# One stage for both Hyena convolutions and the neighbourhood attention, in 64 steps

## The chip, the cores and the metric

The kernel runs on one core of a Trainium2 chip. The metric is the time of the device for one execution, in microseconds. TensorE multiplies matrices, VectorE (DVE), ScalarE (ACT) and GpSimd (POOL) work on elements, SyncE (SP) and POOL issue DMA transfers. The engines meet through semaphores only; each runs its own program in order.

## The reference, cut to what matters

The reference is a chain of two transformer blocks; the change touches the last layer's two mixers. Everything is fp32.

```python
def two_sided_fftconv(u, h_f, h_b):
    kern = jnp.concatenate([h_f, jnp.zeros_like(h_f[:1]), h_b[1:][::-1]], axis=0)
    uf = jnp.fft.rfft(u, n=2 * l, axis=1)
    kf = jnp.fft.rfft(kern, axis=0)
    return jnp.fft.irfft(uf * kf[None], n=2 * l, axis=1)[:, :l]
...
        z = v
        for o, g in enumerate((x1, x2)):
            z = g * (two_sided_fftconv(z, filt[:, o, 0], filt[:, o, 1]) + z * hy_bias[o])
```

There are 1024 positions and 512 channels. The second convolution (order 1) takes the result of the first (order 0).

```python
def neighbourhood_attention(q, k, v, k_ctx, v_ctx, rpb):
    s_rows = jnp.einsum('bhrqd,bhrwkd->bhrwqk', qg, k_rows)
    s_win = (s_win + bias[None])...
    s_ctx = jnp.einsum('bhrqd,bhcd->bhrqc', qg, k_ctx)
    p = jax.nn.softmax(jnp.concatenate([s_win, s_ctx], axis=-1).astype(F32), axis=-1)
    out = jnp.einsum('bhrwqk,bhrwkd->bhrqd', p_rows, v_rows) + jnp.einsum('bhrqc,bhcd->bhrqd', p_ctx, v_ctx)
```

The 1024 latent tokens form a grid of 16 rows and 64 columns, in 8 heads of 64. A query sees a window of 8 rows (512 keys, masked to 16 columns by the bias) and 256 context keys. The two mixers do not depend on each other: both read what the stage before (the projection "g_odd") wrote, and the last projection ("proj3") reads both.

## The kernel before

`program` (L3853) runs a list of stages. Each has its own tiles, semaphores and engine programs (`stage`, L34), and ends with a barrier of all engines once its stores have landed. The three stages concerned come one after another, between `odd_stage` and the last `project_stage` (L3913 to L3917).

`conv_stage` (L3443), run twice. The transform is a product with cosine and sine tables. The input z is held as even and odd positions (r = 0, 1), four tiles of 128 each, 512 channels wide. Forward (L3507 to L3517): for each of four blocks f of 128 frequencies, for cosine and sine (n) and both r, four fp32 matmuls of 128x128 by 128x512 accumulate over t; 16 matmuls per f. ScalarE copies the odd sums out of PSUM (L3540); VectorE makes sum and difference (L3548, L3549), multiplies by the filter's spectrum KS (L3559) and combines (L3562, L3563); POOL mixes the results into Y (L3494, L3495). Inverse (L3519 to L3530): for each of four t and both r, eight fp32 matmuls over f and n; TensorE waits for `mixed` before the first. VectorE adds the bias term (L3572, L3576) and multiplies by the gate (L3578); POOL stores (L3500). The result goes to HBM as Z1, and the second convolution loads it from there. SP loads one table of 1 MB per f or t, in two buffers.

`na_stage` (L3596). Keys and queries of all heads are loaded and transposed first (L3689, L3736, L3738). Then 64 steps: one step u is one grid row of one pair of heads. The queries of both heads stand block-diagonally in a 128x128 tile `qbd` (L3762), so that one matmul of 512 window keys and one of 256 context keys give the scores of both heads (L3703, L3704). VectorE adds the bias (L3787), copies the context scores (L3788) and takes the negated maximum (L3791). ScalarE takes the exponential and its sum (L3751). TensorE transposes the probabilities in six pieces (L3710), ScalarE copies them to SBUF (L3748), TensorE weighs the values in six matmuls of 128 columns (L3722, L3724), of which VectorE scales the two diagonal blocks (L3799) by the reciprocal sum (L3805). Step u of the first part runs with u-1 of the second and u-2 of the third; PSUM holds two score tiles (`pS`). The loop is a hardware loop (`Fori`), with addresses worked out in registers. SP stores after every 16 rows (L3674).

Other stages of the kernel serve as price lists below: the FFN stage (`ffn_up_stage`, L1552 to L1602), the first fused stage (`in_stage`, which runs window attention beside a projection, unrolled; L1206 to L1463), and the RWKV stage (`rwkv_stage`), whose matmuls use half of the array: `halves` are partitions 0 to 63 and 64 to 127, and neighbouring matmuls of L2948, L2960, L2969 and L2972 take turns between them:

```python
BY_TILE = [(h + 4 * (g ^ turn), g) for turn in range(2) for h in range(HN // 2) for g in range(2)]
...
for h, g in BY_TILE:
    op = pe.matmul(C(X_ps[halves[g]], h), A[halves[g], a, h, 0, halves[g]], known, start=True, stop=True)
```

`C` puts heads 0 to 3 into one PSUM bank and 4 to 7 into the next. L2977 does the same with one tile only.

## Time and profile before

| | us |
|---|---|
| median of 3 runs (lowest, highest) | 5161.02 (5156.95, 5164.03) |
| span of the profiled execution | 5162.0 |
| first convolution, from its first load to the next stage's | 143.4 |
| second convolution | 143.5 |
| attention | 363.7 |
| last projection | 142.0 |
| TensorE busy, of the span | 4361.7 |

The profiled execution has no time of its own beside its span, which runs from its first to its last instruction; it stands 1 us above the median. Times of rows are counted from the span's start. Engines: PE is TensorE's matmul, PEld its weight load, SPq and POOLq the queues that issue DMAs. A line of a timeline gives start, duration, engine, source line, operation, tiles written and read, form, and the number of instructions merged in it. An fp32 matmul shows as two records, and one rounded to fp32r as one. A record lasts longer than the distance to the next, since matmuls are pipelined. One record alone lasts 0.59 us at 512 columns in fp32, 0.39 us at 512 in fp32r, 0.27 us as a transpose, 0.28 us at 64 moving columns and full width, and 0.22 us as a 64x64 tile.

### The profile page before, as it was taken

The numbers are of one execution on the slowest core, as the hardware profiler recorded it, in microseconds if no ns is written. First come the engines' busy times: TensorE is split into PE (matmuls) and PEld (weight loads), VectorE is DVE, ScalarE is ACT, GpSimd is POOL, SyncE is SP. The second block draws the span as 40 slices with busy tenths as digits, with TensorE's granted clock in tenths as the row PEclk, the third lists the DMA queues.
The fourth block names the chain that finished last, engine by engine and source line by source line (L and its number), as shares of the span: only waits on it lengthen the run. The fifth ranks groups of instructions, "written<-read, shape, count | busy, mean of one in ns | idle before, by whom it ended". The sixth has DMA issues, their size and how long they took to land. (4 is left out here: it accounts for less than half of the span.)

```text
span 5162.0 us, 69954 instructions
## 1 busy us (share of the span) xinstructions
PE 4361.7 (84%) x25962; PEld 3585.6 (69%) x25962; DVE 2677.9 (52%) x4967; ACT 1488.6 (29%) x3046; POOL 640.9 (12%) x716
## 2 busy tenths in 40 slices
PE   5999998866999995999764769999867998886867
PEld 3998886655888784999762338888757997334546
DVE  3567773754434377111076866677443354444655
ACT  3233322632222254111042423344333111003333
POOL 1111111310000000000030121111121143110001
PEclk8999998887999998999985889999778998998998
DMA  4544442431111344222124754343243354333014
GB/s 155 169 142 139 135 131 111 159 127 58 49 45 44 92 158 137 80 85 86 59 77 156 277 176 107 92 111 107 65 143 120 115 191 176 105 138 91 8 41 139
DMA packets 415931, 593.16 MB, mean 115 GB/s; under 512 B 173209, under 2 KB 306194, under 8 KB 410980
## 3 DMA queue, kind: packets, MB, share of 16 engines
q1 hardware_dynamic: 367961, 422.60, 26.5%
q0 software_dynamic: 46080, 164.57, 8.5%
q8 instruction: 169, 2.77, 0.2%
q10 hardware_dynamic: 1616, 2.36, 0.1%
q14 instruction: 105, 0.85, 0.1%
HBM read 431.77 MB, written 157.67 MB: 114 GB/s over the span
## 5 line engine op out<-in xcount | busy, mean ns | idle before, releaser
L320 PE MATMUL g_in_g_acc<-g_in_g_whi,g_in_hi 128*128 128x444 f32 (+4 forms) x960 | 357.3, 372 | 15.8 <-DVE g_in_g_wlo L310 9.9
L321 PE MATMUL g_in_g_acc<-g_in_g_wlo,g_in_hi 128*128 128x444 f32 (+4 forms) x960 | 346.5, 361 | 0.0
L322 PE MATMUL g_in_g_acc<-g_in_g_whi,g_in_lo 128*128 128x444 f32 (+4 forms) x960 | 346.2, 361 | 0.0
L196 PE MATMUL g_even_acc<-g_even_w_hi,h_hi 128*128 128x384 f32 (+1 forms) x960 | 317.2, 330 | 19.5 <-DVE g_even_w_lo L238 19.5
L199 PE MATMUL g_even_acc<-g_even_w_hi,h_lo 128*128 128x384 f32 (+1 forms) x960 | 317.1, 330 | 0.0
L198 PE MATMUL g_even_acc<-g_even_w_lo,h_hi 128*128 128x384 f32 (+1 forms) x960 | 317.1, 330 | 0.0
L320 PE MATMUL g_odd_g_acc<-g_odd_g_whi,h_hi 128*128 128x344 f32 (+3 forms) x816 | 263.3, 323 | 30.7 <-DVE g_odd_g_wlo L310 16.1
L322 PE MATMUL g_odd_g_acc<-g_odd_g_whi,h_lo 128*128 128x344 f32 (+3 forms) x816 | 261.9, 321 | 0.0
L321 PE MATMUL g_odd_g_acc<-g_odd_g_wlo,h_hi 128*128 128x344 f32 (+3 forms) x816 | 261.8, 321 | 0.0
L1597 DVE SCALAR_TENSOR_TENSOR up_cv<-up_acc,up_taps,up_cv 128x1023 f32<-128x1023 f32 x88 | 112.8, 1282 | 280.8 <-ACT up_cv L1573 273.6
L214 DVE COPY g_even_o_buf<-g_even_acc 128x384 f32<-128x384 f32 (+1 forms) x60 | 32.1, 535 | 399.2 <-PE g_even_acc L199 399.2
L1552 PE MATMUL up_acc<-h_hi,up_w_hi 128*128 128x512 f32 x704 | 220.6, 395 | 8.7 <-DVE up_w_lo L1590 8.7
L320 PEld LDWEIGHTS g_in_g_acc<-g_in_g_whi,g_in_hi 128*128 128x128 f32 x960 | 183.6, 191 | 55.3 <-issue 27.7
L1552 PE MATMUL up_acc<-h_hi,up_w_lo 128*128 128x512 f32 x704 | 219.0, 392 | 0.0
L1552 PE MATMUL up_acc<-h_lo,up_w_hi 128*128 128x512 f32 x704 | 218.4, 391 | 0.0
L1401 DVE SCALAR_TENSOR_TENSOR g_in_m_acc<-g_in_m_w,g_in_c_act,g_in_m_acc 128x256 f32<-128x256 f32 x448 | 201.9, 482 | 22.3 <-issue 1.9
L196 PEld LDWEIGHTS g_even_acc<-g_even_w_hi,h_hi 128*128 128x128 f32 x960 | 181.5, 189 | 19.9 <-DVE g_even_w_lo L238 19.9
L322 PEld LDWEIGHTS g_in_g_acc<-g_in_g_whi,g_in_lo 128*128 128x128 f32 x960 | 183.4, 191 | 7.6
L321 PEld LDWEIGHTS g_in_g_acc<-g_in_g_wlo,g_in_hi 128*128 128x128 f32 x960 | 183.8, 191 | 6.6
L320 PEld LDWEIGHTS g_odd_g_acc<-g_odd_g_whi,h_hi 128*128 128x128 f32 x816 | 156.2, 191 | 38.9 <-DVE g_odd_g_wlo L310 16.5
L198 PEld LDWEIGHTS g_even_acc<-g_even_w_lo,h_hi 128*128 128x128 f32 x960 | 181.5, 189 | 0.0
L199 PEld LDWEIGHTS g_even_acc<-g_even_w_hi,h_lo 128*128 128x128 f32 x960 | 181.4, 189 | 0.0
(564 smaller groups left out, 10281.0 us busy)
## 6 DMA issues: line engine op xcount, KB each, us to landing
down_raw<-in_w_down SPq DMA_DIRECT2D x66, 512.0 KB
g_in_m_w<-in_ada_w SPq DMA_DIRECT2D x24, 1024.0 KB, 5.5
up_w_buf<-in_w_up SPq DMA_DIRECT2D x44, 512.0 KB
U2p<-g_even_o_buf POOLq DMA_DIRECT2D x11, 1920.0 KB, 7.8
g_odd_x<-U3p SPq DMA_DIRECT2D x24, 768.0 KB
g_even_w_buf<-in_even_w_in SPq DMA_DIRECT2D x11, 1536.0 KB
g_in_m_w<-in_w_ada SPq DMA_DIRECT2D x16, 1024.0 KB, 6.0
prep_near<-U2p SPq DMA_DIRECT2D x18, 896.0 KB
```

The lines of the kernel that those rows point to most:

```text
L196: mm = pe.matmul(o, hi[:, k, tt], w_hi[:, par, k, :wd], start=k == 0, stop=not split and k == kc - 1)
L198: pe.matmul(o, hi[:, k, tt], w_lo[:, par, k, :wd], start=False, stop=False)
L199: mm = pe.matmul(o, lo[:, k, tt], w_hi[:, par, k, :wd], start=False, stop=k == kc - 1)
L214: op = eng.tensor_copy(o_buf[:, par, t, :wd], acc[bank][:, :wd])
L320: pe.matmul(bank[:, :wd], hi[:, k, tt], w_hi[:, st % 2, k, :wd], start=k == 0, stop=False)
L321: pe.matmul(bank[:, :wd], hi[:, k, tt], w_lo[:, st % 2, k, :wd], start=False, stop=False)
L322: op = pe.matmul(bank[:, :wd], lo[:, k, tt], w_hi[:, st % 2, k, :wd], start=False, stop=k == KC - 1)
L1401: dve.scalar_tensor_tensor(acc, w, c_act[:, k, c:c + 1], acc, ALU.mult, ALU.add)
L1552: op = pe.matmul(acc[par][side][:, cols], wt[:, par, side, k, :], ht[:, k, cols], start=k == 0 and wt is w_hi and ht is hi, stop=k == KC - ...
L1597: dve.scalar_tensor_tensor(cv[:, side, lag:], acc[par][side][:, :SEQ - lag], taps[:, tap, col], cv[:, side, lag:], ALU.mult, ALU.add)
```

## The change

`conv_stage` (both calls) and `na_stage` go; `hyena_na_stage` replaces them. The tables gain one more layout of the forward transform, `t_fwdb`, in blocks of 256 KB. Step `at` (0 to 63, and three more to drain) has on each engine, in this order:

- TensorE: scores of row `at`; transposes of the probabilities of row at-1; in steps 3 to 11 of each 16, transposes of one pair of key or query tiles for the next pair of heads; convolution block `at`; weighing of row at-1.
- VectorE: result of row at-2; maximum of row `at` (`limit`); output of the convolution; spectrum work, spread over four or five steps.
- ScalarE: copy of the odd sums; copy of the transposed probabilities of row at-1; copy of the key pair; exponentials of row `at`; rounding of table at+1.
- POOL: table_low of block at+1 (table minus its rounded part); mix of a spectrum; the bias term of the convolution; stores of the output and, every 8 rows, of the attention.
- SP: table at+3, spectrum factors, gates, keys, biases and values of the next pair of heads.

Blocks 0 to 15 and 32 to 47 are forward ones (one f, n and r), 16 to 31 and 48 to 63 inverse ones (half of the frequencies of one output tile). z and the forward tables are split in a rounded part and a remainder (fp32r), as the projections of this kernel do it, and a product is the sum of three; the inverse stays fp32. z of the second convolution is made in SBUF and does not pass through HBM. There is one score tile in PSUM, so the scores of a row wait for the exponentials of the row before (`probs`). The maximum is taken over context scores and biased window scores, the latter in one VectorE instruction that also writes the biased scores. Everything is unrolled.

```diff
-                pe.matmul(pS[par][:, 0:WK], qbd[:, par], kT[:, bass.ds(col + start * GRID_C + CTX, WK)], start=True, stop=True)
-                pe.matmul(pS[par][:, WK:NK], qbd[:, par], kT[:, bass.ds(col, CTX)], start=True, stop=True).then_inc(s.s_mm, 1)
...
+            def scores(u):
+                hp, r, start, _ = place(u)
+                if r == 0:
+                    pe.wait_ge(s.kq, PAIRS * (hp + 1))
+                if u:
+                    pe.wait_ge(s.probs, u)
+                for lo, hi, col in ((0, WK, CTX + start * GRID_C), (WK, NK, 0)):
+                    for a in range(2):
+                        e = slice(a * HD, (a + 1) * HD)
+                        op = pe.matmul(pS[e, lo:hi], qT[e, hp % 2, r * GRID_C:(r + 1) * GRID_C], kT[e, hp % 2, col:col + hi - lo], start=True, stop=True)
+                op.then_inc(s.s_mm, 1)
...
+            def turn_p(u):
+                pe.wait_ge(s.probs, u + 1)
+                if u:
+                    pe.wait_ge(s.p_out, u)
...
+            def weigh(u):
...
+                pe.wait_ge(s.p_out, u + 1)
+                if u:
+                    pe.wait_ge(s.y, u)
...
+                for c in range(NP_):
+                    v = vl[:, hp % 2, tile + c] if c < WK // P else vc[:, hp % 2, c - WK // P]
+                    for a in range(2):
+                        e = slice(a * HD, (a + 1) * HD)
+                        op = pe.matmul(pV[e], pT[:, c, e], v[:, e], start=c == 0, stop=c == NP_ - 1)
...
+            def convolve(c):
+                b = block_at(c)
+                if b.f is not None:
...
+                    pe.wait_ge(s.t_lo, forward_at(c) + 1)
...
+                    for k in range(NT // 2):
+                        pe.matmul(bank[:], t_hi[:, k], zh[:, b.r, k], start=k == 0, stop=False)
+                        pe.matmul(bank[:], t_hi[:, k], zl[:, b.r, k], start=False, stop=False)
+                        op = pe.matmul(bank[:], t_lo[:, k], zh[:, b.r, k], start=False, stop=k == NT // 2 - 1)
+                else:
+                    pe.wait_ge(w_in(c), (c // 4 + 1) * DMA)
+                    pe.wait_ge(s.mixed, FCH * b.order + 2 * b.half + 2)
...
+                    for f in range(2):
+                        for n in range(2):
+                            op = pe.matmul(acc[b.q % 3][:], inv(c)[:, f, n], Y[:, 2 * b.half + f, b.r, n], start=b.half == 0 and f == 0 and n == 0, stop=b.half == 1 and f == 1 and n == 1)
...
+            def step(at):
+                if at < NU:
+                    scores(at)
+                if 1 <= at <= NU:
+                    turn_p(at - 1)
+                hp, r = divmod(at, GRID_R)
+                if hp + 1 < HP and TURN_FROM <= r < TURN_FROM + PAIRS:
+                    turn_pair(hp + 1, r - TURN_FROM)
+                if at < NB_:
+                    convolve(at)
+                if 1 <= at <= NU:
+                    weigh(at - 1)
```

On the other engines:

```diff
+            def expose(u):
+                par = u % 2
+                act.wait_ge(s.neg_max, u + 1)
+                act.activation(sc[:, par, 0:WK], sc[:, par, 0:WK], ACT.Exp, scale=-1.0, bias=nm[:, par, 1:2], accum_out=sm[:, par, 0:1])
+                act.activation(sc[:, par, WK:], pS[:, WK:NK], ACT.Exp, bias=nm[:, par, 1:2], accum_out=sm[:, par, 1:2])
...
+            def limit(u):
...
+                dve.tensor_reduce(nm[:, par, 0:1], pS[:, WK:NK], AX_X, ALU.max, negate=True)
+                dve.drain()
+                b = bias[:, hp % 2, off:off + WIN_R].rearrange("p a c -> p (a c)")
+                dve.tensor_tensor_reduce(sc[:, par, 0:WK], pS[:, 0:WK], b, -1.0, nm[:, par, 0:1], ALU.add, ALU.min, nm[:, par, 1:2])
...
+            def table_low(c):
+                pool.wait_ge(s.t_hi, forward_at(c) + 1)
+                pool.tensor_tensor(tl[:, c % 2], w[:, c % 4], th[:, c % 2], ALU.subtract).then_inc(s.t_lo, 1)
...
+                for i in range(2 * FCH):
+                    f = i % FCH
+                    if at == spectrum_end(*divmod(i, FCH)) + (3 if f == FCH - 1 else 5):
+                        mix(i)
```

In `program`:

```diff
-        for order, (zin, zout) in enumerate(((VX[:, 0:HYW], Z1), (Z1, Z2))):
-            conv_stage(nc, f"conv{order}", T["t_fwd"], T["t_inv"], zin, KS[order], VX[:, (order + 1) * HYW:(order + 2) * HYW], T["hy_bias_2"][0, order], zout)
-        na_stage(nc, ident, U3, KV3, BIAS, NA)
+        hyena_na_stage(nc, ident, T["t_fwdb"], T["t_inv"], VX, KS, T["hy_bias_2"][0], Z2, U3, KV3, BIAS, NA)
```

## Rows read from the trace of the kernel before

**Rows 1.** The page, its first part: busy us (share of the span) x instructions.
```profile
...
PE 4361.7 (84%) x25962; PEld 3585.6 (69%) x25962; DVE 2677.9 (52%) x4967; ACT 1488.6 (29%) x3046; POOL 640.9 (12%) x716
...
```

**Rows 2.** Busy times of the three replaced stages; columns in the first line.
```profile
...
core 0: us, PE busy (x) PEld busy (x) DVE busy (x) ACT busy (x) POOL busy (x), PEclk, DMA share, GB/s
4369.40:4512.80 143.40, 117.08 (x256) 50.88 (x256) 57.72 (x80) 4.78 (x8) 22.79 (x20) 0.89 0.37 134
4512.80:4656.30 143.50, 116.69 (x256) 50.64 (x256) 57.73 (x80) 4.78 (x8) 22.81 (x20) 0.89 0.37 134
4656.30:5020.00 363.70, 270.23 (x1480) 185.61 (x1480) 198.19 (x516) 128.33 (x206) 0.00 (x0) 0.96 0.14 36
...
```

**Rows 3.** PE and PEld busy (x), clock, DMA: line L3529, then L1552, in 40 us.
```profile
...
4460.00:4500.00 40.00, 40.00 (x94) 17.67 (x93) 1.00 0.35 119
...
1290.00:1330.00 40.00, 40.00 (x177) 32.81 (x176) 1.00 0.18 51
...
```

**Rows 4.** Waits of the first convolution: who <- for whom, us, times, longest.
```profile
...
PE conv_acc L3516 <- DMA conv_w<-in_t_fwd: 16.7, 1, 16.7
...
```

**Rows 5.** Timeline of the stage edges: start us, us, engine, line, xcount.
```profile
...
4512.77 0.93 SPq L3467 DMA_DIRECT2D conv_z<-Z  x2
...
4525.08 3.75 PE L3516 MATMUL conv_acc<-conv_z,conv_w 128*128 128x512 f32 x4 [18.39 <-DMA conv_w<-in_t_fwd]
...
4693.70 2.05 PE L3703 MATMUL na_pS<-na_kT,na_qbd 128*128 128x512 f32 x2 [8.87 <-DMA na_vl<-U3p]
...
5013.58 0.58 DVE L3799 TENSOR_SCALAR na_y<-na_pV,na_sm 64x64 f32<-64x64 f32 x2 [1.51 <-PE na_pV L3724]
...
5019.96 0.34 SPq L432 DMA_DIRECT2D proj_x<-Z  x1
...
```

**Rows 6.** Timeline of one attention row on TensorE.
```profile
...
4820.63 0.87 PE L3710 MATMUL na_pP<-ident,na_sc 128*128 128x128 f32 x6 [0.16 <-ACTq L3752]
...
4821.56 1.15 PE L3722 MATMUL na_pV<-na_vl,na_pT 128*128 x8
...
4822.55 0.61 PE L3724 MATMUL na_pV<-na_vc,na_pT 128*128 x4
```

**Rows 7.** Waits of the attention loop.
```profile
...
ACT na_sc L3751 <- DVEq L3792: 133.8, 61, 11.6
...
```

**Rows 8.** Timeline of half-size tiles in the RWKV stage, TensorE.
```profile
...
3115.39 0.60 PE L2948 MATMUL rwkv_f<-rwkv_arT,rwkv_bT 64*128 64x256 f32 x4
3115.82 0.60 PE L2948 MATMUL rwkv_f<-rwkv_arT,rwkv_kT 64*128 64x256 f32 x4
...
3117.99 0.60 PE L2948 MATMUL rwkv_f<-rwkv_arT,rwkv_kT 64*128 64x256 f32 x4
3118.52 1.15 PE L2960 MATMUL rwkv_wx<-rwkv_T,rwkv_A 64*64 64x64 f32 x32
...
3126.11 1.14 PE L2977 MATMUL rwkv_wx<-rwkv_T,rwkv_A 64*64 64x64 f32 x16
...
```

**Rows 9.** Busy times in one stretch of full-width records with 64 moving columns.
```profile
...
251.40:253.10 1.70, 1.70 (x17) 1.70 (x16) 0.00 (x0) 0.95 (x2) 0.54 (x1) 1.00 1.06 370
...
```

**Rows 10.** Groups by line and shape: xcount, busy us, mean ns, idle before.
```profile
...
L3751 ACT ACTIVATE na_sc<-na_sc,na_mx 128x768 f32<-128x768 f32 x64 | 59.8, 935 | 137.9 <-DVEq L3792 137.9
...
L3748 ACT ACTIVATE na_pT<-na_pP 128x768 f32<-128x768 f32 x64 | 51.9, 811 | 68.0 <-PE na_pP L3710 68.0
...
L1590 DVE TENSOR_TENSOR up_w_lo<-up_w_buf,up_w_hi 128x2048 fp32r<-128x2048 f32 x22 | 50.4, 2293 | 21.9 <-ACT up_w_hi L1565 14.8 <-issue 7.1
...
L3787 DVE TENSOR_TENSOR na_sc<-na_pS,na_bias 128x512 f32<-128x512 f32 x64 | 44.3, 691 | 71.0 <-PE na_pP L3710 60.1 <-PE na_pS L3704 9.8 <-issue 1.0
...
L1565 ACT ACTIVATE up_w_hi<-up_w_buf 128x2048 fp32r<-128x2048 f32 x22 | 41.9, 1904 | 19.1 <-DMA up_w_buf<-in_w_up 19.1
...
L3494 POOL TENSOR_TENSOR conv_Y<-conv_prod 128x512 f32<-128x512 f32 x16 | 21.1, 1320 | 136.7 <-DVEq L3564 136.7
...
```

**Rows 11.** Busy times of the kernel's own fused, unrolled stage.
```profile
...
260.00:780.00 520.00, 510.11 (x3084) 460.36 (x3084) 371.13 (x863) 156.57 (x416) 61.07 (x113) 0.99 0.42 136
...
```

More of the change, by code:

```diff
@@ L3593, in na_tables, with hyena_na_stage @@
     return hot.reshape(2 * WIN_C, GRID_C * GRID_C)
-def na_stage(nc, ident, U3, KV3, BIAS, NA):
+FWD_BLOCKS, CONV_BLOCKS = 4 * FCH, 8 * FCH
+TURN_FROM, PAIRS = 3, 9
+INVERSE = [(q, h) for h in range(2) for q in range(3)] + [(q, h) for q in range(3, 8) for h in range(2)]
+Block = namedtuple("Block", "order f n r q half t")
+def hyena_na_stage(nc, ident, t_fwdb, t_inv, VX, KS, hy_bias, ZO, U3, KV3, BIAS, NA):
     NR = 2 * WIN_R - 1
@@ new lines, in _, with mix, weigh, store_rows @@
+            in_order(step)
+        @block.gpsimd
+        def _(pool):
+            def mix(i):
+                order, f = divmod(i, FCH)
+                pool.wait_ge(s.prod, i + 1)
+                a = first[:, i % 2]
+                for n in range(2):
+                    pool.tensor_tensor(Y[:, f, 0, n], a[:, 0, n], a[:, 1, n], ALU.add)
+                    pool.tensor_tensor(Y[:, f, 1, n], a[:, 0, n], a[:, 1, n], ALU.subtract)
+                pool.drain()
+                pool.sem_inc(s.mixed, 1)
+            def weigh(order, q):
+                t, r = q // 2, q % 2
+                m = 8 * order + q
+                if order == 0 and q == 0:
+                    pool.wait_ge(s.b_row, 2 * DMA)
+                pool.wait_ge(s.z_lo, 10 if order else 2)
+                if m >= 2:
+                    pool.wait_ge(s.y_done, m - 1)
+                pool.tensor_tensor(zb[:, q % 2], zh[:, r, t], zl[:, r, t], ALU.add)
+                pool.drain()
+                pool.tensor_tensor(zb[:, q % 2], zb[:, q % 2], b_row[:, order], ALU.mult)
+                pool.drain()
+                pool.sem_inc(s.zb, 1)
+            def table_low(c):
+                pool.wait_ge(s.t_hi, forward_at(c) + 1)
+                pool.tensor_tensor(tl[:, c % 2], w[:, c % 4], th[:, c % 2], ALU.subtract).then_inc(s.t_lo, 1)
+            def store_rows(n):
+                hp, half = divmod(n, 2)
+                na_v = NA.rearrange("(r q) c -> q r c", q=GRID_C)
+                pool.wait_ge(s.y, 8 * n + 8)
@@ new lines, in parts, with products @@
+            def parts(order, f, n):
+                m = 8 * order + 2 * f + n
+                dve.wait_ge(s.odd_out, m + 1)
+                dve.tensor_tensor(zz[:, 0, n], acc[2 * n][:], odd[:, n], ALU.add)
+                dve.tensor_tensor(zz[:, 1, n], acc[2 * n][:], odd[:, n], ALU.subtract)
+                dve.drain()
+                dve.sem_inc(s.read, 1)
+            def products(i, a, n):
+                if n == 0:
+                    dve.wait_ge((s.ks_even, s.ks_odd)[a], (i + 1) * DMA)
+                if n == 0 and a == 0 and i >= 2:
+                    dve.wait_ge(s.mixed, i - 1)
+                (zc, zs), (kc, kz) = (zz[:, a, 0], zz[:, a, 1]), (ks[:, a, 0], ks[:, a, 1])
+                dve.tensor_tensor(first[:, i % 2, a, n], zc, (kc, kz)[n], ALU.mult)
+                op = dve.tensor_tensor(second[:, n], zs, (kz, kc)[n], ALU.mult)
+                if n == 1:
+                    op.then_inc(s.ks_read, 1)
@@ new lines, in step @@
+            def step(at):
+                if at >= 2 and at - 2 < NU:
+                    result(at - 2)
+                if at < NU:
+                    limit(at)
+                if at - 1 in outputs:
+                    output(*outputs[at - 1])
+                if at - 2 in outputs and outputs[at - 2][0] == 0:
+                    keep_low(outputs[at - 2][1])
+                spectra(at)
+            for r in range(2):
+                dve.wait_ge(s.z_hi, r + 1)
+                dve.tensor_tensor(zl[:, r], staged(r), zh[:, r], ALU.subtract).then_inc(s.z_lo, 1)
```

625 lines of the change are left out of this document (340 added, 285 removed).

## The prediction, made before the change was run

> **What bounds the kernel now.** The page first: TensorE is busy 84% of the span [rows 1], so the question is where the other 16% lies. The busy times of the stretches put much of it in the three stages that the change replaces: 143.4, 143.5 and 363.7 us, 650.6 us together, with a granted clock of 0.89 in the convolutions and 0.96 in the attention [rows 2]. The reader is to see that a busy share overstates: matmul records last longer than the distance between them, so I count work by start-to-start distances. A 512-wide fp32 matmul is two records; in the inverse transform 94 records touch 40 us, each 0.59 us long, so one comes every (40 + 0.59)/94 = 0.43 us [rows 3]. A convolution has 256 records, 110 us of its 143. The rest is edges: TensorE waits 16.7 us for the first tables [rows 4], and stores, barrier and reload stand between stages: the second convolution's first load is issued at 4512.8 and its first matmul starts at 4525.1 [rows 5].
>
> Attention is bound otherwise. In the timeline of one row, six transposes start 0.12 us apart (0.87 us less one duration of 0.27, over five), and the twelve weighing records come every 0.125 us [rows 6]; with the four score records (two of 0.43, two of half that) that is 1.3 + 0.72 + 1.5 = 3.5 us. The loop runs from 4693.7 to 5013.6 [rows 5], 5.0 us a row. The waits say what fills the gap: ScalarE waits 133.8 us for VectorE's maximum [rows 7]; score, maximum, exponential, transpose, copy and weighing form a ring that TensorE cannot fill. So the old stages hold 2 x 110 + 64 x 3.5 = 444 us of TensorE work in 650.6 us. About 206 us are edges and ring. That is the most that merging alone could give.
>
> **The change, by parts.** *Forward transform.* A block was, in effect, four fp32 matmuls (eight records, 3.45 us) and becomes twelve rounded ones. The FFN stage has these at width 512: 177 in 40 us at 0.39 us each, one every 0.228 us [rows 3]. So 2.75 us, 0.7 less, on 32 blocks. *Inverse transform.* Still eight records, 3.45 us, on 32 blocks.
>
> *Scores.* The block-diagonal query (one 128x128 load) becomes two half-size tiles, each 64 partitions to 64 partitions, with twice the records (eight). If the two tiles stream beside each other, the records start skewed (the second tile's first record beside the first tile's second) and take 4 x 0.43 = 1.72 us; if not, 4 x 0.43 + 4 x 0.215 = 2.59 us. For streaming beside: in the RWKV stage pairs in different 64-row halves run four 256-wide records every 0.43 us (3115.39 to 3115.82), where one at a time would take 0.86; and 64x64 records come at (1.15 - 0.22)/31 = 0.030 us when tiles alternate and (1.14 - 0.22)/15 = 0.061 us when they don't [rows 8]. But those pairs write different banks of PSUM; here both write the same bank, in different partitions. I take 1.72. The Trainium skill, "TensorEngine Tiling (Array Packing)", Gotcha 1, says different row tiles cannot access one PSUM bank at the same time; by that the scores would be the 2.59. No row of before shows such a pair.
>
> *Weighing.* Six matmuls become twelve on two column halves, 24 records, 64 wide. Bounds: 0.030 us each (tiles hide each other) and 0.116 us, the pace of full-width records with 64 moving columns, (1.70 + 0.28)/17 [rows 9]. I take the single tile's 0.061, since here both tiles take the same 128 rows: 1.46 us. The Trainium skill, "TensorE: Matmul & The Clock Gate", Part 3, says a weight load overlaps a running matmul only where the row group differs, which would put each load in front of its matmul. The row disagrees: at 0.116 us a record with a load twice as wide as here, all on one row group, no room is left for a stream of 0.053 us behind each load.
>
> *Transposes.* 6 x 0.12 = 0.72 us, as before; 27 pairs of key and query transposes are moved into steps, 27 x 0.3 = 8 us. *Changes of tile shape*, three a step: the last 64x128 record starts near 3118.31 and the first 64x64 one at 3118.52 [rows 8], 0.1 us more than the spacing. 0.35 us a step with the start of each group.
>
> A forward step is 1.72 + 0.72 + 2.75 + 1.46 + 0.35 = 7.0 us, an inverse one 7.7 us; 32 of each make 470, with the key pairs 478 us.
>
> *Is anything slower than that?* Scores of a row wait for the exponentials of the row before. After the scores, VectorE needs a maximum of 256 and the fused add-and-minimum of 512. The fused instruction is not in the trace; at least 0.69 us, by the add [rows 10], at most about twice that, as separate add and reduction. ScalarE needs two exponentials with their sums, for the one of 0.94 us on 768 columns: 1.5 us. Together some 3.1 us, while TensorE has 5.3 us of transposes, convolution and weighing ahead of the next scores: 2 us of slack. Queued ahead of the maximum on VectorE is the spectrum work of the step before, four instructions of about 0.69 us at most. It hides. The copy of the transposed probabilities (0.81 us) and its handshakes hide under the convolution block. ScalarE's rounding of the table (0.6, under the 0.81 of a wider copy) and POOL's remainder (1.3) come 2 us before they are needed. On eight steps POOL first mixes a spectrum, 4 x 1.3 us, and I allow 7 for contention: the next remainder then comes 1 us early. Totals over the stage: VectorE about 260, ScalarE 200, POOL 130 us: cover enough. Without it (a step of under 6 us) POOL would show. SP issues table, keys, values and bias in one order, each about three steps ahead; its waits on the table and on the spectrum factors hold the next table for at most a step. POOL's attention and result stores (24 issues of 0.5 to 1 us) wait only for rows finished a step earlier.
>
> *Edges.* Start: keys and queries in 512-byte rows go first, then z; 13.5 us, by the 12.3 us of [rows 5] and 1.2 for the keys. Then two roundings of 2048 (1.90 us each) and the last remainder (2.29) [rows 10], with the first maximum and exponentials 9.3 us more; step 1 begins at 23, as if step 0 began at 16. End: transpose, copy, weighing and scaling of the last row 4.4 us, then 6.9 for the store, by 5013.58 to 5019.96 [rows 5]. So 16 + 478 + 11 = 505. The kernel's own fused stage, unrolled like this one, has TensorE busy 510.1 of 520 us at clock 0.99 [rows 11]; that 2% of waits adds 9. The new stage is 514 us, the gain 650.6 - 514 = 137 us. Of it some 22 us are the rounded matmuls, less 27 for the skewed scores. The rest are waits. 5162.0 - 137 = 5025 us; the medians of the runs stand 1 us under the profiled span, so 5024 to 5025 there.
>
> **Rivals.** *Scores one tile at a time*: 0.87 us more on each of 64 steps, 56 us, 5081. For it: nothing in the trace has two tiles in one bank. Against it: disjoint partitions. *Weighing at the alternating pace* of 0.030 us: 24 x 0.031 x 64 = 48 us less, 4977; for it the RWKV rows, against it the shared rows of the array, and POOL's mix that would then be late. *Weight loads in front of each matmul*: half of 0.116 for the load and 0.053 for the stream, 0.111 us a record, 77 us more, 5102. That is the page's rule on overlap. *VectorE or POOL late*: the remainder or the maximum arrives behind the spectrum work, 1 us on each of the 32 forward steps, 5057; the trace has single POOL and VectorE instructions stretched, but the slack is 1 to 2 us. *Slower than before*: every weighing record finishes before the next starts, since the tile changes at each, 0.218 us instead of 0.061 [rows 8]: 24 x 0.157 x 64 = 241 us more, 5266. It decides from 0.061 + 137/1536 = 0.15 us a record. Against it: alternating tiles are the fastest records of the trace. *The change does not fill the waits* at all would be the ring of 5.0 us plus 3.1 us of block in each step, 8.1 us, 518 instead of 470, 5073; its chance is part of that of late helpers.
>
> **Numbers.** Chances: forecast 0.60, scores in turn 0.15, fast weighing 0.10, late helpers 0.07, loads in front 0.05, slower 0.03. The forecast's own range is 5005 to 5045 (edges 5 us, unseen waits 0 to 4%). The range over the cases is 4970 to 5100. A measurement here tells 0.2%, 10 us: faster 0.96, same 0.01, slower 0.03.
>
> **What would show it.** One stage of about 514 us before the last projection; steps of 7.0 and 7.7 us; TensorE without waits of over 1 us but at the first steps; eight score records in 1.9 us (2.6 if in turn); weighing records 0.061 us apart; the exponentials 3 us behind the scores. A ScalarE or POOL release in TensorE's waits would prove the slack wrong, as would a step over 8 us.

## The result, and the profile after

The changed kernel takes 4954.81 us (median of 4 runs, 4947.8 to 4962.18) against 5162.52 of the kernel before (4 runs, 5156.95 to 5169.88): ratio 0.9596, 95% interval 0.9581 to 0.9612. The prediction was 5025 with a range of 4970 to 5100. The direction was right; the gain is 208 us where 137 was forecast, and the time lies 15 us below the range.

The page's first part, and the busy times of the new stage from its first DMA issue to that of the next stage (they answer to [rows 1] and [rows 2]):

```profile
PE 4270.7 (86%) x27114; PEld 3547.5 (72%) x27114; DVE 2633.8 (53%) x4845; ACT 1526.3 (31%) x3235; POOL 741.6 (15%) x796
```

```profile
core 0: us, PE busy (x) PEld busy (x) DVE busy (x) ACT busy (x) POOL busy (x), PEclk, DMA share, GB/s
4371.20:4813.00 441.80, 410.21 (x3144) 246.06 (x3144) 269.03 (x554) 176.34 (x410) 146.76 (x120) 0.98 0.37 108
```

Three stages of 650.6 us became one of 441.8, 208.8 less; all of the gain is here. 514 was forecast. The profiled span is 4956.0 us, 1 us above the median of the runs.

One forward step on TensorE (start, us, line, tiles, count), with the beginning of the next:

```profile
4402.11 1.51 PE L3715 MATMUL mix_pS<-mix_kT,mix_qT 64*64 64x512 f32 x8
4403.55 0.88 PE L3723 MATMUL mix_pP<-ident,mix_sc 128*128 128x128 f32 x6
4404.19 0.48 PE L3771 MATMUL mix_acc<-mix_zh,mix_th 128*128 128x512 f32 x1
4404.50 0.39 PE L3772 MATMUL mix_acc<-mix_zl,mix_th 128*128 128x512 f32 x1
...
4407.11 0.69 PE L3749 MATMUL mix_pX<-mix_vl,mix_pT 128*64 128x64 f32 x16
4407.63 0.40 PE L3749 MATMUL mix_pX<-mix_vc,mix_pT 128*64 128x64 f32 x8
4407.96 1.51 PE L3715 MATMUL mix_pS<-mix_kT,mix_qT 64*64 64x512 f32 x8
```

The distances from the start of one group to the start of the next are scores 1.44 us, transposes 0.64, block 2.92, weighing 0.85, together 5.85 where 7.0 was forecast. Each distance holds its group's records and what the change to the next group's tile shape takes. Within the first weighing group a record comes every (0.69 - 0.22)/15 = 0.031 us; the one row of [rows 8] with that pace is the alternating one. An inverse step, from the same view:

```profile
4488.83 1.51 PE L3715 MATMUL mix_pS<-mix_kT,mix_qT 64*64 64x512 f32 x8
4490.27 0.88 PE L3723 MATMUL mix_pP<-ident,mix_sc 128*128 128x128 f32 x6
4490.98 3.60 PE L3786 MATMUL mix_acc<-mix_Y,mix_w 128*128 128x512 f32 x8
4494.51 0.69 PE L3749 MATMUL mix_pX<-mix_vl,mix_pT 128*64 128x64 f32 x16
4495.02 0.40 PE L3749 MATMUL mix_pX<-mix_vc,mix_pT 128*64 128x64 f32 x8
4495.36 1.51 PE L3715 MATMUL mix_pS<-mix_kT,mix_qT 64*64 64x512 f32 x8
```

6.53 us, where 7.7 was forecast. A key pair's transposes make a step 0.22 us longer. TensorE's waits in the stage (who, for whom, us, times, longest):

```profile
PE mix_pS L3806 <- DMA mix_kst<-U3p: 11.5, 1, 11.5
PE mix_acc L3771 <- POOL mix_tl L3670: 8.5, 5, 7.1
PE mix_pS L3715 <- ACTq L3852: 3.6, 4, 1.3
PE mix_pX L3731 <- DVE mix_y L3911: 3.2, 2, 1.8
PE mix_acc L3771 <- DVE mix_zl L3960: 1.4, 1, 1.4
```

The first is the loading of keys, and 7.1 us of the second the first table; both belong to the start, which takes 25.1 us to the scores of row 1 (4371.19 to 4396.26). What is left, 9.6 us in eleven waits, belongs to the steps. Read by the distances between score groups, the excess of late steps over their kind is 11.8 us: the eleventh step of each convolution (7.68 and 8.09 us where 6.07 is usual), the steps around the turn from forward to inverse, and the second step of the second convolution (7.55).

The sum of the stage is thus 25.1 + 401.3 (scores of row 1 to those of row 63) + 6.5 (step 63) + 8.9 (last row, store, end) = 441.8.

A part of the gain that the prediction did not price is TensorE's granted clock, the third figure from the end of these lines. Before, it was still at the lower of its two levels (0.50, 1.2 GHz) when work resumed after a wait, here at the start of the first convolution; in the changed stage it stands at the upper one (2.4 GHz) from row 1 on:

```profile
4381.20:4386.00 4.80, 4.80 (x6) 2.16 (x7) 0.00 (x0) 0.00 (x0) 0.00 (x0) 0.50 1.03 434
```

```profile
4397.00:4808.00 411.00, 399.18 (x3104) 238.05 (x3100) 263.45 (x549) 166.55 (x397) 140.91 (x117) 1.00 0.32 96
```

A 512-wide fp32 record lasts 1.06 us at the lower level and 0.59 at the upper. By the distances between starts, an estimate: 56 records of the three stages of before ran at the lower level and cost about 16 us more than at the upper one; in the changed stage 26 did, all at its start, for about 4 us. So some 12 of the 208.8 us come from a clock that stays up because TensorE no longer waits. No run separates this share.

### The profile page after: what moved, and what is told of

The parts are those of the page before. It is cut to its first block and busy times, and to the rows that moved or that the text cites. A ratio compares the mean times of both kernels' runs of the same rounds, so it can differ in the third digit from the quotient of the medians.

```text
span 4956.0 us, 70950 instructions
## 1 busy us (share of the span) xinstructions
PE 4270.7 (86%) x27114; PEld 3547.5 (72%) x27114; DVE 2633.8 (53%) x4845; ACT 1526.3 (31%) x3235; POOL 741.6 (15%) x796
## 5 line engine op out<-in xcount | busy, mean ns | idle before, releaser
L1552 PE MATMUL up_acc<-h_hi,up_w_hi 128*128 128x512 f32 x704 | 220.4, 395 | 8.5 <-DVE up_w_lo L1590 8.5
L1552 PE MATMUL up_acc<-h_hi,up_w_lo 128*128 128x512 f32 x704 | 218.6, 392 | 0.0
L1552 PE MATMUL up_acc<-h_lo,up_w_hi 128*128 128x512 f32 x704 | 218.2, 391 | 0.0
```

Of the source, the lines that this page charges most:

```text
L1552: op = pe.matmul(acc[par][side][:, cols], wt[:, par, side, k, :], ht[:, k, cols], start=k == 0 and wt is w_hi and ht is hi, stop=k == KC - ...
```

## The experiments

Stage lengths below run from the stage's first DMA issue to that of the stage after it, in the profiled execution; the rest of the span varied by up to 16 us from one kernel to the next although its code was the same, so where an edit is worth few us the stage length decides. There is one profile of each kernel, two of the changed one (441.8 and 442.3 us).

**The control**, the changed kernel again.

> The changed kernel itself, as a control beside the runs that follow. Both theories: its new stage takes 442 us again from its first DMA issue to that of the next stage, 24 weighing records at a mean step of 0.031 us in the groups that run one behind the other, eight score records in 1.44 us.

4951.57 us, ratio 0.9598 (0.9582 to 0.9614), stage 442.3. The same again.

**Weighing without turns.**

```diff
-                for c in range(NP_):
-                    v = vl[:, hp % 2, tile + c] if c < WK // P else vc[:, hp % 2, c - WK // P]
-                    for a in range(2):
-                        e = slice(a * HD, (a + 1) * HD)
+                for a in range(2):
+                    e = slice(a * HD, (a + 1) * HD)
+                    for c in range(NP_):
+                        v = vl[:, hp % 2, tile + c] if c < WK // P else vc[:, hp % 2, c - WK // P]
                         op = pe.matmul(pV[e], pT[:, c, e], v[:, e], start=c == 0, stop=c == NP_ - 1)
```

> The weighing's 12 matmuls per row are issued as six for the left 64 columns of the array and then six for the right 64, in place of left and right in turn; number, shape and operands stay. Theory A (two matmuls on different column halves of the array hide each other's fixed part, so that a turn-by-turn order takes half the time): with the turn taken away the records start 0.061 us apart, as in the attention rows of before, the weighing takes 24 x 0.061 = 1.5 us in place of 0.84, each of 64 steps grows by 0.65, and the kernel is 40 us or so slower (4995). Theory B (a 64 wide tile on 128 partitions is fast by its form alone, whatever stands beside it): the records stay 0.031 apart and the time stays within 3 us of 4955.

4976.49 us, ratio 0.9644 (0.9628 to 0.966), stage 466.9, 25 us longer. The timeline of one weighing:

```profile
4402.02 0.68 PE L3749 MATMUL mix_pX<-mix_vl,mix_pT 128*64 128x64 f32 x8
4402.54 0.22 PE L3749 MATMUL mix_pX<-mix_vc,mix_pT 128*64 128x64 f32 x1
4402.54 0.27 PE L3749 MATMUL mix_pX<-mix_vl,mix_pT 128*64 128x64 f32 x1
4402.60 0.22 PE L3749 MATMUL mix_pX<-mix_vc,mix_pT 128*64 128x64 f32 x1
...
4403.06 0.40 PE L3749 MATMUL mix_pX<-mix_vc,mix_pT 128*64 128x64 f32 x4
4403.39 1.51 PE L3715 MATMUL mix_pS<-mix_kT,mix_qT 64*64 64x512 f32 x8
```

Theory A holds in kind, at 25 us for the 40 expected: without turns a record comes every 0.057 us and the weighing takes 1.37 us. It is less than the 1.5 expected because the right side does not wait for the left one to end. The row at 4402.54 that lasts 0.27 us is the right side's first record (a tile's first record is the longer one), and it starts together with the left side's ninth of twelve. From there on, for some slots, two run at once. The step grows by 0.5 us; of 64 x 0.5 = 32 us, 8 are taken back because longer steps leave the helpers more time: TensorE's waits within steps are 2.8 us in three places here, and the one for the first table is 1.3 us shorter.

**Weighing in full width.**

```diff
-                    for a in range(2):
-                        e = slice(a * HD, (a + 1) * HD)
-                        op = pe.matmul(pV[e], pT[:, c, e], v[:, e], start=c == 0, stop=c == NP_ - 1)
+                    op = pe.matmul(pX[:, 2 * P:3 * P], pT[:, c, :], v, start=c == 0, stop=c == NP_ - 1)
```

with two scalings of 64 partitions each behind it.

> The weighing is made of six matmuls over all 128 columns into a 128 wide place of the other bank, of which half is not wanted; the result is taken from it by two instructions of 64 partitions in place of one of 128. Theory A (the narrow form saves the half that is not wanted because left and right run together): 12 records at about 0.125 us, 1.5 us in place of 0.84, so each step grows by 0.6 to 0.7 and the kernel is 38 to 45 us slower. Theory B (narrow tiles save nothing over the full form, the gain of the stage lies elsewhere): within 3 us of 4955. The vector engine's added instruction, about 0.2 us per row, has room in either.

4974.58 us, ratio 0.9647 (0.963 to 0.9663), stage 469.5.

```profile
4401.69 1.05 PE L3747 MATMUL mix_pX<-mix_vl,mix_pT 128*128 128x128 f32 x8
4402.57 0.61 PE L3747 MATMUL mix_pX<-mix_vc,mix_pT 128*128 128x128 f32 x4
4403.11 1.51 PE L3715 MATMUL mix_pS<-mix_kT,mix_qT 64*64 64x512 f32 x8
```

Twelve records take 1.42 us, one every (1.05 - 0.27)/7 = 0.111. Theory A in kind, again below the 38 to 45 us expected: the narrow form is worth 28 us of stage, and without turns 25 of them are gone, as the run before shows. The step grows by 0.50 us (6.35 for 5.85) though the weighing takes 0.57 more: the full width has the block's tile shape, and the block's last record is followed after 0.23 us, its usual distance, where 0.32 us pass in the changed kernel.

**Scores without turns.**

```diff
-                for lo, hi, col in ((0, WK, CTX + start * GRID_C), (WK, NK, 0)):
-                    for a in range(2):
-                        e = slice(a * HD, (a + 1) * HD)
+                for a in range(2):
+                    e = slice(a * HD, (a + 1) * HD)
+                    for lo, hi, col in ((0, WK, CTX + start * GRID_C), (WK, NK, 0)):
```

> The four score matmuls of a row are issued as both of the upper tile (rows and columns 0 to 63) and then both of the lower one, in place of upper and lower in turn for each of the two key ranges. Theory A (matmuls start in the order of the queue, one waits for the one ahead on its own tile, and only neighbours in the queue on different tiles run together): the second upper matmul holds back the first lower one, so that only the middle pair overlaps, and the scores take 0.21 + 0.44 + 0.21 and so on, 2.1 to 2.4 us in place of 1.44; each of 64 steps grows by 0.6 to 0.9 and the kernel is 40 to 60 us slower. Theory B (a tile that is free takes its matmul whatever stands before it in the queue): 1.44 stays, and the time is within 3 us of 4955.

4946.24 us, ratio 0.9593 (0.9577 to 0.9609), stage 442.3: no change. The rival that scores go one tile after another is answered by the same row:

```profile
4405.45 1.51 PE L3715 MATMUL mix_pS<-mix_kT,mix_qT 64*64 64x512 f32 x8
4406.90 0.33 PE L3723 MATMUL mix_pP<-ident,mix_sc 128*128 128x128 f32 x1
```

1.45 us for eight records of which the four of one tile alone are 2 x 0.43 + 2 x 0.215 = 1.29 us of stream. In the 0.05 us behind 4405.45 two records are already under way:

```profile
4405.45 0.65 PE L3715 MATMUL mix_pS<-mix_kT,mix_qT 64*64 64x512 f32 x2
```

Both tiles stream from the first record on, although the lower tile's first record stands fifth in the queue. So theory A as I put it (neighbours only) is wrong, and yet the weighing without turns lost half of its overlap. What reconciles them is how far the engine looks. In the weighing by six, the right side's first record, the thirteenth in the queue, began with the ninth, four ahead of it; in the scores the lower tile's first record is the fifth, four behind the first. By that the next orders can be foretold.

**Weighing by threes, and by twos.** The one line of the order, `a, c = i // 3 % 2, i // 6 * 3 + i % 3` for i from 0 to 11, and the same with twos.

> The weighing's 12 matmuls (24 records) are issued as three for the left 64 columns, three for the right, three left, three right. In the runs before, score matmuls issued as two upper and two lower (four records each) overlapped in full, while weighing by six (twelve records) overlapped only from the ninth record on. Theory A (a matmul on a free tile may start while at most four records ahead of it in the queue are unfinished, a look-ahead of four): by threes (six records) two records at the beginning and two at the end run alone, 14 slots of 0.057 in place of 12, so the weighing takes 0.84 + 0.11 = 0.95 us, each step grows by 0.11 and the kernel by 5 to 7 us (4961). Theory B (only strict turns overlap, and the scores are a different case by their row tiles): 1.37 us as by six, and 25 us slower (4976).

4955.8 us, ratio 0.96 (0.9586 to 0.9615), stage 449.5, 7.7 us longer than the changed kernel. Theory A. The steps are 6.02 us in place of 5.85: 0.17 us are three slots of 0.057. Two are the lag that was expected; the third is there because the left side's first record takes two slots (0.11 us to the next), so that the right side begins three slots late and not two. The times of whole runs cannot tell 5 to 7 us, the steps can.

> The weighing's matmuls in turns of two for the left and two for the right columns (four records each). Read closely, the runs by six and by three say this: a record on a free tile starts once it is among the four that stand behind the record that has just started. By six the right side began right behind the ninth left record, by three right behind the third, and the scores by two right behind the first. Theory A (four behind): by two nothing is lost but some ends, weighing 0.84 to 0.9 us, step 5.85 to 5.9, stage 442 to 445. Theory B (only neighbours in the queue pair up): half of the pairs are lost, weighing 1.1 to 1.2, stage 455 or more.

4953.17 us (one run), stage 443.8, steps 5.88. Theory A again. Three orders of weighing and one of scores now follow from one statement: a matmul record on a free tile starts once it is among the four records behind the one that last started. All these matmuls are fp32, two records each with their weight loads, so whether the limit counts four records, two matmuls or something else is not shown.

**Two stages.** The new stage as two calls, convolution parts and attention parts. Matmuls, copies and roundings inside are unchanged; what paces SP's loads and the attention's stores had to be another wait.

```diff
-        hyena_na_stage(nc, ident, T["t_fwdb"], T["t_inv"], VX, KS, T["hy_bias_2"][0], Z2, U3, KV3, BIAS, NA)
+        for what in ("conv", "na"):
+            hyena_na_stage(nc, what, ident, T["t_fwdb"], T["t_inv"], VX, KS, T["hy_bias_2"][0], Z2, U3, KV3, BIAS, NA)
...
             def step(at):
-                if at < NU:
+                if na and at < NU:
                     scores(at)
```

> The new stage is run as two: first one with its convolution parts alone, then one with its attention parts alone; every matmul, copy and rounding inside stays as the change made it. It tells what the merging is worth from what the new inner forms are worth. Theory A (the attention row is a ring of engines that wait for each other, and the convolution block is what fills it): the attention stage alone keeps a row every 4.7 us or so, not the 2.9 of its matmuls, and takes 325 us; the convolution stage alone takes its matmuls' 200 us and 40 us of edges and handovers; together 565, so the kernel is about 125 us slower than the changed one (5077), and some 80 us of the 207 gained come from the inner forms alone. Theory B (the gain comes from the inner forms, merging saves little more than one stage edge): within 30 us of 4955.

5093.76 us, ratio 0.9874 (0.9859 to 0.9889). The busy times of the two:

```profile
4360.60:4633.60 273.00, 216.70 (x640) 127.58 (x640) 152.68 (x170) 36.62 (x58) 142.35 (x104) 0.89 0.37 125
4633.60:4946.00 312.40, 219.34 (x2504) 133.15 (x2504) 114.57 (x384) 137.10 (x352) 11.00 (x16) 0.96 0.18 44
```

585.4 us together against 441.8 merged and 650.6 before. Theory A. Running the two side by side is worth 144 us. The convolutions take 273.0 us, 33 more than expected, with TensorE busy 216.7: alone, they too wait for the other engines. The clock has a share in the 144: by the same estimate as above the lower level costs 19 us here and 4 in the merged stage.

The other 65 us are 14 in the convolutions (286.9 to 273.0) and 51 in the attention (363.7 to 312.4). They are not TensorE's forms alone: the two convolutions share one stage and its edges, the attention's first scores come 12 us after its start where it was 37 (one pair of heads is transposed first, not all), and its rows are shorter. Its ring keeps 4.39 us a row (4.67 with a key pair), against 5.0 before, and is seen in one row:

```profile
4702.98 1.51 PE L3724 MATMUL mixna_pS<-mixna_kT,mixna_qT 64*64 64x512 f32 x8 [0.17 <-ACTq L3862]
...
4704.53 0.42 DVE L3907 TENSOR_REDUCE mixna_nm<-mixna_pS 128x1 f32<-128x256 f32 x1 [0.93 <-PE mixna_pS L3724]
4705.07 0.75 DVE L3910 CUSTOM_DVE_ANT_0 mixna_sc<-mixna_pS,mixna_bias,mixna_nm 128x512 f32<-128x512 f32 x1
...
4706.03 0.71 ACT L3860 ACTIVATE mixna_sc<-mixna_sc,mixna_nm 128x512 f32<-128x512 f32 x1
...
4706.74 0.46 ACT L3861 ACTIVATE mixna_sc<-mixna_pS,mixna_nm 128x256 f32<-128x256 f32 x1
...
4707.37 1.51 PE L3724 MATMUL mixna_pS<-mixna_kT,mixna_qT 64*64 64x512 f32 x8 [0.26 <-ACTq L3862]
```

Scores, minimum on VectorE, two exponentials on ScalarE, next scores. A convolution block lies inside this time.

**Short blocks.** `for k in range(NT // 2)` becomes `range(1)` in the forward blocks, and the inverse block has one matmul: the kernel leaves out three quarters of the convolution's matmuls.

> Leaves out most of the convolution: a forward block issues 3 of its 12 matmuls, an inverse block 1 of its 4; every wait, copy and spectrum operation stays. It asks how much of a step the attention row's ring of engines would take with little beside it. Theory A (the ring found in the attention part alone, 4.39 us a row, stands under the step): steps do not go under 4.4, near 4.4 to 4.7 where the vector engine is free and 6 or so where it carries the spectra; stage 310 to 340 us. Theory B (TensorE's sum alone sets the step): 3.7 in a forward and 3.9 in an inverse step, stage 280.

4886.06 us (one run), stage 374.0. Of 63 steps none is under 4.38 us; 17 lie between 4.38 and 4.48, and eleven at 4.66 or 4.67. Where VectorE carries the spectra they are 5.3 to 9.0 us, with VectorE busy 36.1 of the 40 us from 4440 to 4480. The stage is longer than either theory's (310 to 340, and 280), but the floor of the ring is theory A's. A forward step of 5.85 us has 1.46 us of slack over it.

**Forward blocks in fp32.**

```diff
-                        pe.matmul(bank[:], t_hi[:, k], zh[:, b.r, k], start=k == 0, stop=False)
-                        pe.matmul(bank[:], t_hi[:, k], zl[:, b.r, k], start=False, stop=False)
-                        op = pe.matmul(bank[:], t_lo[:, k], zh[:, b.r, k], start=False, stop=k == NT // 2 - 1)
+                        op = pe.matmul(bank[:], table[:, k], zh[:, b.r, k], start=k == 0, stop=k == NT // 2 - 1)
```

and without the splitting of table and sequence.

> The forward blocks go back to plain fp32: eight records per block in place of twelve of the split, and with them go the splitting of table and sequence on the scalar, vector and gpsimd engines. Theory A (the split pays on TensorE and its splitting is hidden): forward block 3.45 us in place of 2.84, so each of 32 forward steps grows by 0.6 and the middle of the stage by 18 to 20 us; the start loses the wait for the first table's low part, 7 us; the kernel is 10 to 13 us slower (4967). Theory B (the splitting work is what holds the engines back): no slower, or faster than 4955 by the waits on the low table, 8.5 us.

4955.56 us, ratio 0.9598 (0.9583 to 0.9613), stage 448.8: whole runs show no difference, and the stage is 7.0 us longer; theory A had the kernel 10 to 13 us slower. A forward step is 6.52 us, so 31 of them behind the start are 21 us longer; but the stretch from row 1 to row 63 is only 10.9 us longer, and the start 4.0 shorter. In this kernel no late step is left: every step is 6.52, 6.53, 6.74 or 6.75 us, but for the first two. So the split gains 21 us on TensorE and gives 14 back, 10 in late steps and 4 at the start.

**Who makes the late steps.** In the changed kernel two VectorE rows of such a place, and what POOL does meanwhile:

```profile
4475.87 1.58 DVE L3936 TENSOR_TENSOR mix_first<-mix_first,mix_second 128x512 f32<-128x512 f32 x1
4477.37 1.75 DVE L3937 TENSOR_TENSOR mix_first<-mix_first,mix_second 128x512 f32<-128x512 f32 x1
```

```profile
4475.19 1.71 POOL L3649 TENSOR_TENSOR mix_Y<-mix_first 128x512 f32<-128x512 f32 x1
4477.25 1.32 POOL L3670 TENSOR_TENSOR mix_tl<-mix_w,mix_th 128x512 fp32r<-128x512 f32 x1 [0.35 <-issue]
```

With nothing on POOL, at 4498.55, the first of them takes 0.69 us. The instruction that loses most is the smallest, the addition of the two exponentials' sums, one column wide:

```profile
L3905 DVE TENSOR_TENSOR mix_rs<-mix_sm 128x1 f32<-128x1 f32 x64 | 36.6, 572 | 98.2 <-PE mix_pX L3749 97.1
```

Alone it takes 0.16 us; 42 of the 64 overlap a POOL instruction and take 0.79 us on average, so that 26 of the 36.6 us are beyond what it takes alone. The edit moves the 32 subtractions `tl = w - th` from gpsimd to the end of VectorE's step.

```diff
             def table_low(c):
-                pool.wait_ge(s.t_hi, forward_at(c) + 1)
-                pool.tensor_tensor(tl[:, c % 2], w[:, c % 4], th[:, c % 2], ALU.subtract).then_inc(s.t_lo, 1)
+                dve.wait_ge(s.t_hi, forward_at(c) + 1)
+                dve.tensor_tensor(tl[:, c % 2], w[:, c % 4], th[:, c % 2], ALU.subtract).then_inc(s.t_lo, 1)
```

> The low part of each forward table is subtracted on the vector engine at the end of its step in place of gpsimd. In the changed kernel 11.8 us of the stage are steps longer than the rest (step 11, and six around the turn from forward to inverse in each convolution), and none is left where the forward blocks are fp32; vector operations that stand beside a gpsimd one there took 1.1 to 1.75 us in place of 0.69. Theory A (the late steps come from gpsimd and the vector engine slowing each other): with the subtraction at 0.7 on the vector engine the longer steps shrink, stage 3 to 8 us shorter (434 to 439). Theory B (they come from the vector engine's load, 90 per cent busy and more in these steps): its 32 added subtractions, 22 us, make them longer, stage 5 to 15 us longer.

4941.24 us, ratio 0.9578 (0.9562 to 0.9594). The busy times of its stage:

```profile
4358.20:4795.10 436.90, 409.73 (x3144) 246.17 (x3144) 270.03 (x586) 176.34 (x411) 99.46 (x88) 0.98 0.37 110
```

Theory A. VectorE has 32 instructions more (586 against 554) and is busy the same 270 us; the one-column additions alone fall from 36.6 to 27.2 us. POOL is busy 47 us less; the stage is 4.9 us shorter. Of the 11.8 us of late steps some 7 remain, and what makes them is not separated: POOL's mixes of the spectra still stand beside VectorE's work. The subtractions were no load that gpsimd took off VectorE: they cost VectorE as much from there.

**The start, in another order.**

```diff
+            load_w(0)
             for r in range(2):
-                sp.dma_start(staged(r), VX[:, 0:HYW].rearrange("(t p r) c -> r p t c", p=P, r=2)[r]).then_inc(s.z_in, DMA)
-                load_w(r)
+                sp.dma_start(staged(r), VX[:, 0:HYW].rearrange("(t p r) c -> r p t c", p=P, r=2)[r]).then_inc((s.z_in, s.z_in_b)[r], DMA)
+            load_w(1)
...
+            act.activation(odd[:, 0, 0:1], ident[:, 0:1], ACT.Exp)
...
+            table_high(0)
             for r in range(2):
+                act.wait_ge((s.z_in, s.z_in_b)[r], DMA)
                 act.activation(zh[:, r], staged(r), ACT.Copy).then_inc(s.z_hi, 1)
-            table_high(0)
```

> The first 25 us of the new stage in another order: the first table is loaded and rounded ahead of the sequence, the two halves of the sequence have a semaphore each, an Exp on one column is issued early so that the scalar engine's table is there, and the first softmax limit comes ahead of the second half's low part. Theory A (the start is a chain through the scalar engine's and gpsimd's roundings): scores of row 1 come 4 to 7 us earlier than 25.1 us after the stage's first DMA issue, the stage takes 435 to 438 us and the kernel 4 to 7 us less (4949), which is near what can be told. Theory B (the start is bound by the key transposes and their DMA): the scores of row 1 stay at 25 us.

4941.84 us, ratio 0.9579 (0.9566 to 0.9592), stage 437.8; the scores of row 1 come 21.0 us after the first DMA issue. Theory A, at the lower end; which part of the edit does it was not separated. On VectorE the first softmax limit also stands ahead of the second half's low part. In the changed kernel the table's rounding stood behind those of the sequence, and its low part on POOL then took 3.24 us beside VectorE's, against 1.27 here, where it is done before they begin:

```profile
4383.86 3.71 ACT L3881 ACTIVATE mix_zh<-mix_Y 128x2048 fp32r<-128x2048 f32 x2 [1.01 <-DMA mix_Y<-VX]
4385.80 4.49 DVE L4006 TENSOR_TENSOR mix_zl<-mix_Y,mix_zh 128x2048 fp32r<-128x2048 f32 x2 [19.04 <-ACT mix_zh L3881]
...
4388.17 3.24 POOL L3670 TENSOR_TENSOR mix_tl<-mix_w,mix_th 128x512 fp32r<-128x512 f32 x1 [20.58 <-ACT mix_th L3835]
```

**Both.**

> The two edits that each shortened the stage, together: the reordered start (stage 437.8 us in place of 442) and the tables' low parts on the vector engine (436.9). They act at different places, the first before the scores of row 1, the second on the late steps from 11 on. Theory A (they add): stage 431 to 434 us, ratio to the kernel before 0.956 or a little under, 4932 to 4938 us. Theory B (the vector engine, which now makes the first low parts too, delays the start again): the scores of row 1 later than 21 us after the first DMA issue and the stage near 437.

4939.71 us (median of 5, 4932.21 to 4947.9), ratio 0.9584 (0.9571 to 0.9597), stage 432.4, row 1 at 20.9 us (expected were a ratio of 0.956 or a little under and a stage of 431 to 434). Theory A: in the stage the two add, 9.4 us together. Against the changed kernel's control ratio of 0.9598 the whole time does not prove it faster, since 9 us are within what the rest of the program varies by; the stage lengths are the evidence, and there is one profile of each.

## Why the prediction was wrong where it was

**What bounds the kernel: right in kind.** Merging was to fill waits and edges, and did: of 650.6 us before, 206 were not TensorE's work by my count; in the new stage 40 are not, where the forecast left 36 (16, 11 and 9). The miss is in TensorE's work itself. It was to grow from 444 to 478 us and fell to 402, which is 32 x 5.85 + 32 x 6.53 and 27 key pairs of 0.22. The run in two stages gives 144 us for running convolution and attention side by side. That this stands near the 142 of the forecast (137, and the 5 by which skewed scores were to outweigh rounded matmuls) is in part luck: the other 65 us of that run hold an edge, a shorter start and a shorter ring, which the forecast had counted among its waits.

**Weighing: wrong, the largest term.** I took 0.061 us a record, "since here both tiles take the same 128 rows". Nothing in the trace supported that reason. The two paces of [rows 8] differ by whether tiles alternate, and here they do; but the tiles there also stand on different rows, so no row of before could decide. 0.031 was measured: 1.46 us for 24 records became 0.74, 46 us over 64 steps. With the turns taken away the pace is 0.057, with full width 1.42 us a row. The rival at the alternating pace (4977) was the true one and was given 0.10. The Trainium skill, "TensorE: Matmul & The Clock Gate", Part 3, says that a weight load overlaps a running matmul only where its row group differs. All these loads use all rows, and each side's records come every 0.057 us with 0.053 us of stream in each, which leaves no room for a load between them; the trace disagrees. So does the run in full width, 0.111 us a record with 0.107 of stream (0.43 x 128/512). The prediction already called [rows 9] a row that disagrees. That reading was wrong: 0.116 us leaves 0.063 for a load in front of 0.053 of stream.

**Scores: the mechanism right, the size off.** Both tiles stream beside each other in one bank of PSUM, but without the skew of one record: 1.29 us of stream for 1.72, 28 us over the stage. (The 1.44 us of the group hold 0.15 of what follows below.) The rule of "TensorEngine Tiling (Array Packing)", Gotcha 1, in the Trainium skill, that different row tiles cannot access one bank at the same time, would have given 2.59; it did not show here, where the two tiles write different partitions.

**Changes of tile shape, with the starts of groups: right.** The 0.35 us a step came from one distance in [rows 8], so that it fits so well is also luck. With the other terms at the pace inside their groups, a forward step is 1.29 + 0.72 + 2.75 + 0.74 = 5.50 us, and it measures 5.85; an inverse one is 6.20 and measures 6.53. What is left, 0.35 and 0.33 us, lies where the shape changes: 0.15 us in the scores' distance, 0.11 in the weighing's, 0.09 or 0.07 in that of transposes and block. The run in full width, which spares one change, agrees: its step grew by 0.07 us less than its weighing.

**Forward and inverse blocks: right.** 0.23 us a record forward for 0.228, and 3.53 us an inverse block for 3.45.

**Helpers hidden: right, with less room.** I gave 2 us of slack and said that without cover of 6 us POOL would show. Steps are 5.85 us, and POOL does show: 1.4 us directly, and through VectorE in at least the 5 of the 11.8 us of late steps that went with its subtractions. The 2% of waits, 9 us, was a fair size with a wrong picture: I expected them spread, they are a dozen steps. The fused instruction, unseen before, takes 0.75 us, near the lower bound; the two exponentials 0.71 and 0.46.

**Edges: near.** Row 1 at 25.1 us for 23; end 8.9 for 11, of which half a microsecond was a misreading (5013.58 to 5019.96 is 6.4 us, not 6.9).

In sum: 470 us for the steps became 32 x 5.85 + 32 x 6.53 = 396, which is the 72 us of the stage but for 2. Weighing (46) and scores (28) are these 74 us. The range failed because its lower end was one rival, 4977, with 7 us for everything else, while the skew of the scores could also come to nothing, and no case took the two together: 5025 - 46 - 28 = 4951.

## What to carry to other kernels

When one stage is a ring of engines and another a stream of TensorE, put a piece of the stream into each turn of the ring; its worth is bounded beforehand by the edges plus the ring's gaps, here 206 us, of which 40 were left. Issue half-array matmuls in turns of at most two (fp32) per tile, because here the overlap ended where the other tile's record was further than four behind. Work moved from VectorE to gpsimd is not free for VectorE: compare the busy time of VectorE with and without it before counting it as hidden. When a sum is built from paces inside groups, the changes between groups need their own term, and they are not to be counted again when the measured distances are compared with it.

## What had not been expected of the hardware

- Two column halves on the same 128 rows overlap fully when they take turns: 0.031 us a record of 64 columns, 0.057 without turns, 0.111 for a full-width one of 128.
- TensorE starts a record on a free tile ahead of older ones on a busy tile, up to four records ahead: by six, three, two and one in turn the weighing took 1.37, 1.02, 0.88 and 0.85 us, and scores in either order 1.44 to 1.45.
- Two 64x64 tiles on different rows and columns, writing different partitions of one bank of PSUM, stream side by side: 1.44 us for the group, with 1.29 us of stream on each.
- VectorE instructions with both inputs in SBUF last 1.58 and 1.75 us beside POOL's, 0.69 alone, and one of a single column up to 1.28 us for 0.16, while the one that reads PSUM kept 0.75 us. 32 subtractions moved onto VectorE left its busy time at 270 us. The Trainium skill, "SBUF — State Buffer", section "SBUF: two separate sides", states that these two engines take a shared pair of ports by turns for whole instructions; the stretched rows agree with it.
